# The second attention's scores: three passes of rounded operands instead of plain fp32 products

## What is computed

```
def block_attention(q, k, v, scale):     # scores = q k^T * scale, softmax, times v
...
q_a = concat(q_nope, q_pe)               # 8 heads, 128 + 64 wide, one key per head
k_a = concat(k_nope, k_pe)               # k_pe is shared by the heads
y_a = block_attention(q_a, k_a, v_a, A_SCALE)
y_b = block_attention(q_b, k_b, v_b, B_SCALE)   # 8 heads of 128, 2 shared keys and values
```

## Time and profile before

| | us |
|---|---|
| Three runs, median | 2447.07 (2444.69 to 2451.93) |
| Profiled execution, from its first to its last instruction | 2445.5 |
| TensorE busy in it | 2382.9 |
| VectorE busy in it | 1665.3 |
| ScalarE busy in it | 1035.3 |

### The profile page before, as it was taken

One profiled execution on the slowest core, in us unless ns is written; L12 is line 12 of the kernel. 1 busy time (PEld: TensorE's weight loads), 2 busy tenths in 40 slices (PEclk: granted clock), 3 DMA queues, 4 the chain that ended last, 5 costly groups with the idle time before them and its releaser, 6 DMA issues.

```text
span 2445.5 us, 38231 instructions
## 1 busy us (share of the span) xinstructions
PE 2382.9 (97%) x15580; PEld 2041.9 (83%) x15580; DVE 1665.3 (68%) x1909; ACT 1035.3 (42%) x1366; POOL 232.5 (10%) x204
## 2 busy tenths in 40 slices
PE   5999999999999999999999999999999999999996
PEld 1688776569888999888998888888789999999995
DVE  8755645456888888887678567555667576667558
ACT  2454864224333433343344455444534333334342
POOL 0139800011000000000020100000004100000000
PEclk7999999999999999999999999999999999999998
DMA  9944579997999999998554764334454566677652
GB/s 389 346 155 155 161 282 380 387 372 261 355 354 352 369 346 343 346 346 300 173 173 145 224 178 138 106 104 132 145 178 126 167 217 243 230 250 245 184 165 114
DMA packets 257855, 589.19 MB, mean 241 GB/s; under 512 B 22673, under 2 KB 30097, under 8 KB 256401
## 3 DMA queue, kind: packets, MB, share of 16 engines
q1 hardware_dynamic: 257680, 586.76, 69.3%
HBM read 584.59 MB, written 2.10 MB: 240 GB/s over the span
## 4 chain that ended last, share of the span: by engine, by line
PE 89%; DVE 4%; DMA 2%; ACT 2%; issue 1%; POOL 1%; SPq 0%; DVEq 0%; ACTq 0%
PE psum L218 13%; PE psum L220 13%; PE psum L219 13%; PE psum L231 12%; PE psum L233 12%; PE psum L232 12%; PE psum L301 3%; DMA start_slots<-in_w_ada 2%; PE psum L2719 1%; PE psum L2043 1%; DVE wlo L207 1%; PE psum L797 1%; PE psum L577 1%; PE psum L527 1%; PE psum L924 1%
## 5 line engine op out<-in xcount | busy, mean ns | idle before, releaser
L207 DVE TENSOR_TENSOR wlo<-raw,whi 128x1024 fp32r<-128x1024 f32 (+2 forms) x720 | 879.7, 1235 | 507.5 <-ACT whi L201 505.2
L201 ACT CAST whi<-raw 128x1024 fp32r<-128x1024 f32 (+2 forms) x720 | 736.1, 1029 | 933.6 <-PE psum L220 468.5
L231 PE MATMUL psum<-hh,whi 128*128 128x256 f32 x2176 | 608.9, 280 | 0.9 <-ACT powers L2595 0.5
L232 PE MATMUL psum<-hh,wlo 128*128 128x256 f32 x2176 | 601.7, 277 | 0.0
L233 PE MATMUL psum<-hl,whi 128*128 128x256 f32 x2176 | 601.6, 276 | 0.0
L231 PEld LDWEIGHTS psum<-hh,whi 128*128 128x128 f32 x2176 | 408.8, 188 | 2.3 <-ACT powers L2595 0.8
L232 PEld LDWEIGHTS psum<-hh,wlo 128*128 128x128 f32 x2176 | 408.9, 188 | 0.8 <-issue 0.5
L233 PEld LDWEIGHTS psum<-hl,whi 128*128 128x128 f32 x2176 | 408.7, 188 | 0.0
L218 PE MATMUL psum<-whi,hh 128*128 128x512 f32 (+1 forms) x720 | 290.3, 403 | 2.6 <-POOL hl L554 1.4
L220 PE MATMUL psum<-whi,hl 128*128 128x512 f32 (+1 forms) x720 | 280.9, 390 | 0.0
L219 PE MATMUL psum<-wlo,hh 128*128 128x512 f32 (+1 forms) x720 | 279.5, 388 | 0.0
(11 more groups left out here) (416 smaller groups left out, 3024.9 us busy)
## 6 DMA issues: line engine op xcount, KB each, us to landing
araw<-in_ada_w SPq DMA_DIRECT2D x132, 512.0 KB, 6.3
raw<-in_w_in_fourier SPq DMA_DIRECT2D x128, 512.0 KB, 4.1
raw<-in_w_ffn_gate SPq DMA_DIRECT2D x88, 512.0 KB, 9.5
raw<-in_w_ffn_up SPq DMA_DIRECT2D x88, 512.0 KB, 7.8
raw<-in_w_ffn_down SPq DMA_DIRECT2D x88, 512.0 KB, 10.7
raw<-in_w_in_attn SPq DMA_DIRECT2D x88, 512.0 KB, 4.4
araw<-in_w_ada SPq DMA_DIRECT2D x80, 512.0 KB, 6.8
start_slots<-in_w_ada SPq DMA_DIRECT2D x64, 512.0 KB, 8.1
```

The costliest lines, as they stand in the source:

```text
L201: nc.scalar.copy(whi[:, u % SPLITS, 0:kn, 0:w], raw[:, u % RING, 0:kn, 0:w]).then_inc(s_hi, 1)
L207: nc.vector.tensor_tensor(wlo[:, u % SPLITS, 0:kn, 0:w], raw[:, u % RING, 0:kn, 0:w], whi[:, u % SPLITS, 0:kn, 0:w].bitcast(F32), ALU.subt ...
L231: nc.tensor.matmul(o, h, mh[:, kt + k], start=(kt + k == 0 and f % 2 == 0), stop=False)
L232: nc.tensor.matmul(o, lw, mh[:, kt + k], start=False, stop=False)
```

## The change

The main part of the scores, plain fp32 before, is formed in three passes of rounded operands, accumulated in the same PSUM bank. For that:

- ScalarE's copies of the turned queries and keys write fp32r tiles (`qT2h`, `kT2h`, `kbTh`), that is, rounded; their number and order stay.
- VectorE subtracts the rounded values from the same PSUM banks and writes the low parts (`qT2l`, `kT2l`) in a new step `head_low_dve`, once per head, and `kbTl` in `k_low_dve`, twice in round 0.
- TensorE's scores, the transposes of the next head and the first unit of the next round wait for these too (`s_tl`), and the first gate product for `s_kbl`.
- The 64-deep rotated part stays plain fp32. The tiles lie in memory that is free at that time; `kbTl` is over the keys in `kvb` that were turned.

```diff
@@ program @@
+    kT2l = sb(a1, "k_low", [P, 512], F32R)
...
+    kbTh = sb(a1, "kb_high", [P, 2, 512], F32R)
...
+    kT2h = sb(a1, "k_high", [P, 512], F32R)
+    qT2h = sb(a1, "q_high", [P, S], F32R)
+    xacc_mid = sb(a1, "q_rope", [P, S])
+    qT2l = sb(a1, "q_low", [P, S], F32R)
...
+    kbTl = sb(a1, "kb_low", [P, 4, 512], F32R)
...
@@ k_turn_act @@
-            ins = nc.scalar.copy(kbT[:, r - 1], psum[:, 8 - r])
+            ins = nc.scalar.copy(kbTh[:, r - 1], psum[:, 8 - r])
         ins.then_inc(s_ke, 1)
 
+
+    def k_low_dve(dve, r):
+        dve.wait_ge(s_ke, r + 1)
+        dve.wait_ge(s_kt, 3)
+        nc.vector.tensor_tensor(kbTl[:, 2 * r - 2:2 * r, 0:256], psum[:, 8 - r].rearrange("p (a b) -> p a b", a=2),
+                                kbTh[:, r - 1].bitcast(F32).rearrange("p (a b) -> p a b", a=2), ALU.subtract).then_inc(s_kbl, 1)
@@ pair_mult @@
                 if i:
-                    pe.wait_ge(s_te, 4 * i)
+                    pe.wait_ge(s_tl, 4 * i)
...
                     pe.wait_ge(s_ke, 3)
+                    pe.wait_ge(s_kbl, 2)
@@ head_turn_pe @@
         if n:
             pe.wait_ge(s_te, n)
+            pe.wait_ge(s_tl, n)
@@ head_scores_pe @@
         pe.wait_ge(s_te, n + 1)
+        pe.wait_ge(s_tl, n + 1)
         if n:
             pe.wait_ge(s_ex2, 2 * n)
+        g = head(i, k) // 4
+        kv = (kT2h[:] if k < 2 else kbTh[:, g]).rearrange("p (a b) -> p a b", a=2)
+        lv = kT2l[:].rearrange("p (a b) -> p a b", a=2) if k < 2 else kbTl[:, 2 * g:2 * g + 2, 0:256]
+        for t in range(TT):
+            a = slice(t * P, t * P + P)
+            o = psum[:, 2 + t].rearrange("p (a b) -> p a b", a=2)
+            nc.tensor.matmul(o, qT2h[:, a], kv, start=True, stop=False)
+            nc.tensor.matmul(o, qT2h[:, a], lv, start=False, stop=False)
+            ins = nc.tensor.matmul(o, qT2l[:, a], kv, start=False, stop=(k >= 2))
         if k < 2:
             for t in range(TT):
-                nc.tensor.matmul(psum[:, 2 + t], qT2[:, 0, t * P:t * P + P], kT2, start=True, stop=False)
-            for t in range(TT):
                 rows = slice(ROPE * t, ROPE * t + ROPE)
-                ins = nc.tensor.matmul(psum[:, 2 + t], qT2[rows, 1, 0:P], kpeT[rows], start=False, stop=True)
-        else:
-            for t in range(TT):
-                a = slice(t * P, t * P + P)
-                ins = nc.tensor.matmul(psum[:, 2 + t], qT2[:, 0, a], kbT[:, head(i, k) // 4], start=True, stop=True)
+                ins = nc.tensor.matmul(psum[:, 2 + t], qrT[rows], kpeT[rows], start=False, stop=True)
         ins.then_inc(s_s2, 1)
@@ head_store_act @@
-        ins = nc.scalar.copy(qT2[:, 0], psum[:, 0, 0:S])
+        ins = nc.scalar.copy(qT2h[:], psum[:, 0, 0:S])
         if k < 2:
-            nc.scalar.copy(qT2[:, 1, 0:P], psum[:, 0, S:S + P])
-            ins = nc.scalar.copy(kT2, psum[:, 1])
+            nc.scalar.copy(qrT, psum[:, 0, S:S + P])
+            ins = nc.scalar.copy(kT2h[:], psum[:, 1])
@@ new, ahead of head_max_dve @@
+    def head_low_dve(dve, i, k):
+        dve.wait_ge(s_te, 4 * i + k + 1)
+        ins = nc.vector.tensor_tensor(qT2l[:], psum[:, 0, 0:S], qT2h[:].bitcast(F32), ALU.subtract)
+        if k < 2:
+            ins = nc.vector.tensor_tensor(kT2l[:], psum[:, 1], kT2h[:].bitcast(F32), ALU.subtract)
+        ins.then_inc(s_tl, 1)
@@ pairs_dve2 @@
                 z_mean_dve(dve, 1)
+                k_low_dve(dve, 1)
+                k_low_dve(dve, 2)
             pair_rope_dve(dve, ch, i)
...
             for s in range(12, 16):
                 pair_low(dve, i, s)
+            head_low_dve(dve, i, 0)
             head_max_dve(dve, ch, i, 0)
             head_norm_dve(dve, i, 0)
             for k in range(1, 4):
+                head_low_dve(dve, i, k)
                 head_pT_dve(dve, i, k - 1)
```

More of the change, by code:

```diff
@@ L128, in program @@
     pad = sb(ctx, "pad", [P, 16])
+    a1 = ExitStack()
+    kbTh = sb(a1, "kb_high", [P, 2, 512], F32R)
+    a1.close()
     powers = sb(ctx, "powers", [P, 2, CW])
@@ L135, in program @@
     x = sb(ctx, "x", [P, TT, D])
+    a1 = ExitStack()
+    xacc_front = sb(a1, "xacc_front", [P, 2816])
+    kT2h = sb(a1, "k_high", [P, 512], F32R)
+    qT2h = sb(a1, "q_high", [P, S], F32R)
+    xacc_mid = sb(a1, "q_rope", [P, S])
+    qT2l = sb(a1, "q_low", [P, S], F32R)
+    a1.close()
     xacc = sb(ctx, "xacc", [P, TT, D])
@@ L2183, in program @@
     rope_b = condf[:, 512:1024].rearrange("p (t n) -> p t n", t=TT)
-    kbT = powers
     qp = xaf[:, 0:512].rearrange("p (t h e) -> p t h e", t=TT, h=2)
@@ L2187, in program @@
     kvp = xaf[:, 768:2816].rearrange("p (t n) -> p t n", t=4)
-    kT2 = xaf[:, 2816:3328]
-    qT2 = xaf[:, 3328:3840].rearrange("p (h s) -> p h s", h=2)
+    qrT = xaf[:, 3584:3584 + P]
     prob2 = arawf[:, 0:1024].rearrange("p (t s) -> p t s", t=TT)
@@ L2209, in program @@
         "turned", "stored", "scores", "max", "exp", "recip", "p_turned", "pT_act", "pT_dve", "pv", "y"))
+    s_tl, s_kbl = sem("a2_low"), sem("k_low")
     s_nrm, s_yh2, s_yl2 = sem("a2_normed"), sem("y2_high"), sem("y2_low")
```

## The result

| | before | after |
|---|---|---|
| Median of 5 runs, us | 2447.07 (2444.69 to 2451.93) | 2463.66 (2463.42 to 2465.51) |
| Profiled execution, span, us | 2445.5 | 2463.6 |

The change makes the kernel slower: ratio 1.0081, 95% interval 1.0070 to 1.0092. The forecast was 2469.0 with a range of 2456 to 2477. The two medians of the table stand 16.6 us apart, which is 1.0068 and under this interval. The first of them is high: in 54 later runs the kernel before had a median of 2443.4, and against that the change costs 20.3 us, 1.0083.

A forecast was written before the change was run, and what follows sets the result against it. TensorE, full from end to end in the second attention, was taken as the bound. Median 2447.07 plus 14.1 us (+13.6 + 0.4 - 2.2 + 2.3) plus 7.8 for the clock gave 2469.0 us, range 2456 to 2477.

The forecast's parts named there:

- head 0: later start of the scores, four rounds: TensorE waits 3.65 us for VectorE's low parts in each round, plus 0.1 for the first product after the wait.
- gate product: First gate product, once: waits for the shared keys' low parts on VectorE, +2.3 us.
- clock behind head 0's waits: TensorE's clock falls to half for 3.9 us after each of four waits, 1.95 us lost each, +7.8 us.
- clock behind the gate product: After the 2.3 us wait before the first gate product, no loss from a fall of the clock was taken.
- all sixteen heads' passes, no waits: TensorE's scores: three rounded passes replacing each plain product save 0.35 us (heads 0, 1) or 0.27 (2, 3), -5.0 us.
- TensorE's order is full, so everything added counts: Second attention: TensorE busy 239.4 of 241.1 us, so added work or waits go straight into the time.
- VectorE's low parts stand behind unit 15: VectorE's queue: head 0's subtractions follow unit 15, done at 1587.4, where TensorE is ready at 1583.77; 3.65 us wait.
- Head 1, +0.1 each: Head 1's scores: wait 0.35 plus 0.1 less gain 0.35 us, four times, +0.4 us in all.
- Heads 2 and 3 covered: Low parts ready 1 us before TensorE wants them, so no wait; eight times -0.27, -2.2 us.
- The clock that held behind head 0's waits: Rival: TensorE's clock does not fall after the waits, time 2461.2 us; chance 0.30.
- The low parts that come early: Rival: head 0's low parts done before TensorE wants them, all waits vanish, -5.0 us, 2442.1; chance 0.03.
- the passes at 131 ns each: Rival: TensorE's rounded passes stream at the skill page's pace, -9.2 us on rows alone, 2459.8; chance 0.02.

The follow-up runs named there:

- e3: The changed kernel with 14 extra rounded products on TensorE filling the wait for head 0's low parts; 2457.95 against 2443.30 us for the kernel before.
- e2: e1 with ScalarE also storing head 0's operands ahead of rounding unit 14; 2443.47 against 2443.30 us for the kernel before.
- e5: e2 with the scores' main part as plain fp32 products, low parts formed and waited for but left out; 2452.43 against 2443.69 us for the kernel before.
- e1: The changed kernel with VectorE's low parts of head 0 behind unit 13 instead of unit 15; 2446.23 against 2443.30 us for the kernel before.
- e8: The changed kernel with the keys' low part of head 0 subtracted twice in each round; 2468.68 against 2443.40 us for the kernel before.
- e9: The changed kernel run again unaltered, beside runs of the kernel before; 2464.84 against 2443.40 us.
- e4: The kernel before plus only a TensorE wait for unit 15's low part ahead of head 0's scores; 2458.42 against 2443.30 us for the kernel before.

## Why the prediction held, step by step

The sum was +14.1 us at full clock and +7.8 for the clock, 21.9. The attention in the trace after costs 22.45.

| term | predicted | measured |
|---|---|---|
| head 0: later start of the scores, four rounds | 14.6 to 15.0 | 14.3 (3.54, 3.58, 3.59, 3.59) |
| heads 0 to 3 net at full clock, four rounds | 11.8 | 11.1 (e3) |
| gate product | 2.3 | 2.3 |
| clock behind head 0's waits | 7.8 | 7.5 (after less e3) |
| clock behind the gate product | 0 | 1.5 in this execution, 0 to 2.8 in the others |
| all sixteen heads' passes, no waits | -5.0 | -5.6 (e2 less e5) |

- *TensorE's order is full, so everything added counts:* held. 22.45 us at the end of the attention were still there at the end of the kernel.
- *VectorE's low parts stand behind unit 15:* shown by e1 (take the place away, and 19 of 22 us go) and e8 (lengthen the chain by 0.69 us, and the wait grows by 0.72). The 3.65 us were 3.6; the operations took 0.42 and 0.68, and overlap by about 0.1.
- *Head 1, +0.1 each:* in e3 0.1. *Heads 2 and 3 covered:* no wait there in any trace, 0.25 to 0.35 us gained in e3.
- *The clock falls after each of the four waits:* it did, in all twelve waits of the changed kernel, of its repetition and of e8. The price of 1.95 us, taken from the time between the first dense product and the rise of the clock in the earlier trace rows, came out at 2.3, 1.5, 1.5 and 2.3. That the four add up to 7.5 for 7.8 is in part luck: the price took one low stretch of 3.9 us for each wait, and they lasted 3.4 us twice and 6.8 us twice.
- *None for the gate product:* a term put at nothing without a reason. With the same code up to there and a wait of 2.8 us the clock fell in three executions (after, e1, e9), at 1.5 to 2.8 us each, and held in four (e2, e3, e5, e8). Over the seven that is 0.8 us on average, so the forecast lost little by it.
- *The time itself* came out 5.3 us under the forecast. Most of this, 3.6 us, is the base: "I add to the median". The 2447.07 stood on few runs, and the profiled execution of before had itself lost over 4 us to the fall of the clock at 396 us. In 54 further runs the kernel before had medians of 2443.3, 2443.7 and 2443.4; eight of the 54 took over 2446.0 us, of the first five three did. That those three held such a fall is likely, but not shown. From 2443.5 the same sum gives 2465.4, against 2463.66 and 2464.84 measured. The rest is the sum: 21.9 us, where the medians differ by 20.2 and 21.4. The own costs of 22.45 and 23.2 are those of the two profiled executions, which at 2465.37 and 2470.19 us were slower than the medians of their kernel. The row was read as a price for the new waits; that the same row was also 4 us of the base that a next execution need not have was not drawn from it.
- *Rivals.* The clock that held behind head 0's waits in all four rounds is e3, where the wait is filled, and in e4 it held in one round of four. The low parts that come early are e1 and e2, which I made; the passes at 131 ns each, as the Trainium skill has it ("TensorE: Matmul & The Clock Gate", "Back-to-back issue gap"), did not show: 0.23 us in every trace. The columns split in two times 256 cost nothing: 0.23 us is also the pace of the unsplit weight products.

What stays open: what decides, at one and the same wait of 2.6 or 2.8 us, whether the clock falls. Behind the gate product it is not the program, since executions of the same code differ. Among thin work shorter waits can be enough: in e9 the clock fell at 394 us, between two waits of 1.4 us.

## What to carry to other kernels

Where one engine's order is full, price a new step on another engine by its place in that engine's queue, not by its length: 1.1 us of subtraction behind a unit that came late anyway cost 3.6 us of TensorE each time, the same 1.1 us two units earlier 0.6 (e1), and nothing once ScalarE's store came earlier too (e2). A stall of TensorE is to be priced with a fall of its clock behind it: here it fell behind all 12 waits of 3.4 us or more and behind 6 of 11 of 2.5 to 2.8, and the waits of head 0 cost half as much again. And before a forecast is added to a measured time, look whether that time holds such an event of its own.

## What was not expected

- The saving of three rounded passes over a plain fp32 product is small: 1.47 against 1.72 us for 2 x 512 columns, 0.25 us per head, since each pass stands at 0.23 and the step between operand types takes about 0.09.
- A bare wait of 2.6 us costs 2.9 us when the clock holds and 4.3 to 5.5 when it falls (e4).
- Filling a wait with products that nobody needs made the kernel 6 to 7 us faster than leaving TensorE idle (e3, 2457.95, against 2463.66 and 2464.84).
